# Decoder trunk on one core: dense tiles of 1408 and 1344 rows, B parts at other steps, half of a w_out product in three parts

## The reference

```
h = rmsnorm(x); z = h @ w_in            # 1024 -> 3 * 512
ya = S5 state-space mixer of z[:, :512] # B, C, recurrence, GELU, per-group GLU
yb = gated unit of z[:, 512:]
x = x + [rmsnorm(ya), rmsnorm(yb)] @ w_out
h = rmsnorm(x)
layer 1: x = x + (silu(h @ w_gate) * (h @ w_up)) @ w_down   # 2752 hidden
layer 2: x = x + top-2 of 8 experts, each a SwiGLU with 1376 hidden
```

## Time and profile before

| | us or share |
|---|---|
| median of the runs | 855.05 |
| the profiled execution, its own time | 856.37 |
| its span, from first to last instruction | 854.5 |
| TensorE (PE) busy | 812.2, 95% |
| VectorE (DVE) busy | 557.7, 65% |
| ScalarE (ACT) busy | 401.2, 47% |
| GpSimd (POOL) busy | 209.2, 24% |
| mean DMA rate | 235 GB/s |

### The profile page before, as it was taken

How to read it: one execution, slowest core, us unless ns; L and a number is a source line. 1 busy time by engine, 2 the same in 40 slices (tenths; PEclk the granted TensorE clock), 3 DMA queues, 4 the chain that set the end, 5 groups by cost and what they waited for, 6 DMA issues and landing times.

```text
span 854.5 us, 13785 instructions
## 1 busy us (share of the span) xinstructions
PE 812.2 (95%) x5080; PEld 631.7 (74%) x5080; DVE 557.7 (65%) x1006; ACT 401.2 (47%) x608; POOL 209.2 (24%) x182
## 2 busy tenths in 40 slices
PE   9999999999999969999999998998999998999994
PEld 7487779999999969848777887886876442865322
DVE  8999577566478871577952799799846131964115
ACT  7885455364332331377341587676734021750102
POOL 3801132223354111525112002414214000131002
PEclk9999999999999989999999899999999999999999
DMA  9603535554653431650410498987999999999993
GB/s 300 201 1 140 217 101 192 164 173 142 188 154 93 147 117 50 200 153 4 153 53 1 176 421 305 360 302 253 381 390 384 422 420 421 422 413 422 422 413 127
DMA packets 89474, 200.77 MB, mean 235 GB/s; under 512 B 26256, under 2 KB 48032, under 8 KB 89408
## 3 DMA queue, kind: packets, MB, share of 16 engines
q1 hardware_dynamic: 88480, 198.86, 63.5%
q10 hardware_dynamic: 576, 0.59, 0.2%
q0 software_dynamic: 352, 0.44, 0.2%
HBM read 198.25 MB, written 1.61 MB: 234 GB/s over the span
## 4 chain that ended last, share of the span: by engine, by line
PE 57%; DVE 20%; DMA 8%; issue 5%; SPq 5%; ACT 3%; POOL 1%; DVEq 0%; ACTq 0%; POOLq 0%
PE ps L1335 6%; PE ps L1336 6%; PE ps L1337 6%; PE ps L1539 5%; SPq L771 4%; PE ps L1345 4%; PE ps L1667 3%; PE ps L1651 3%; PE ps L1652 3%; PE ps L1654 3%; DVE D L1851 2%; DMA wraw_d<-in_moe_w_gate 2%; DMA wraw_g<-in_moe_w_down 2%; DMA wraw_g<-in_moe_w_gate 2%; PE ps L1429 2%
## 5 line engine op out<-in xcount | busy, mean ns | idle before, releaser
L1335 PE MATMUL ps<-Md,split_u 128*128 128x288 f32 (+2 forms) x304 | 89.7, 295 | 0.0
L1337 PE MATMUL ps<-Md,split_u 128*128 128x288 f32 (+2 forms) x304 | 89.1, 293 | 0.0
L1851 DVE TENSOR_TENSOR xb<-xb,ps 128x288 f32<-128x288 f32 x80 | 33.3, 450 | 70.8 <-PE ps L1539 26.6
L831 POOL TENSOR_TENSOR wrnd_g<-wraw_g,wrnd_g 128x1024 fp32r<-128x1024 f32 (+1 forms) x6 | 17.0, 2835 | 177.2 <-ACT wrnd_g L1012 177.2
L1851 DVE TENSOR_TENSOR wrnd_g<-wraw_g,wrnd_g 128x1376 fp32r<-128x1376 f32 (+2 forms) x31 | 48.9, 1597 | 13.8 <-ACT wrnd_g L1012 13.6
L1851 DVE TENSOR_TENSOR wrnd_u<-wraw_u,wrnd_u 128x1376 fp32r<-128x1376 f32 (+2 forms) x34 | 57.8, 1732 | 0.0
L1336 PE MATMUL ps<-hbr,split_u 128*128 128x288 f32 (+1 forms) x192 | 57.1, 297 | 0.0
L1337 PEld LDWEIGHTS ps<-Md,split_u 128*128 128x128 f32 (+2 forms) x304 | 56.9, 187 | 0.0
L1335 PEld LDWEIGHTS ps<-Md,split_u 128*128 128x128 f32 (+2 forms) x304 | 56.8, 187 | 0.1
L1851 DVE TENSOR_TENSOR wrnd_d<-wraw_d,wrnd_d 128x1376 fp32r<-128x1376 f32 (+2 forms) x20 | 31.8, 1620 | 34.1 <-ACT wrnd_d L1012 34.1
L1006 ACT ACTIVATE split_u<-raw 128x1024 fp32r<-128x1024 f32 (+2 forms) x38 | 39.5, 1047 | 30.0 <-PE ps L1337 30.0
(11 more groups left out here) (472 smaller groups left out, 2171.9 us busy)
## 6 DMA issues: line engine op xcount, KB each, us to landing
wraw_g<-in_moe_w_gate SPq DMA_DIRECT2D x31, 688.0 KB, 11.2
wraw_u<-in_moe_w_up SPq DMA_DIRECT2D x29, 688.0 KB, 17.0
wraw_d<-in_moe_w_gate SPq DMA_DIRECT2D x22, 688.0 KB, 9.1
wraw_g<-in_moe_w_down SPq DMA_DIRECT2D x28, 512.0 KB, 15.2
wraw_u<-in_moe_w_down SPq DMA_DIRECT2D x28, 512.0 KB, 13.7
raw<-in_ffn_w_gate SPq DMA_DIRECT2D x20, 512.0 KB, 4.6
raw<-in_ffn_w_up SPq DMA_DIRECT2D x20, 512.0 KB, 4.2
raw<-in_ffn_w_down SPq DMA_DIRECT2D x20, 512.0 KB, 3.8
```

The costliest lines, as they stand in the source:

```text
L1335: pe.matmul(out, w_hi, x_hi, start=start, stop=False)
L1337: return pe.matmul(out, w_lo, x_hi, start=False, stop=stop)
L1851: return dve.tensor_tensor(o, a, b, op)
```

## The change

- The first half of the hidden rows is 1408 (eleven full tiles), the second 1344 (ten and 64 rows). In the second half's last tile, gate and up weights stand side by side in one split slot (64 columns each) and go through one product of 128 output rows. VectorE takes the gate from partitions 0 to 63 and up from 64 to 127.
- In the last down chunk (64 rows) the high weights are copied a second time to partitions 64 to 127, and the low part of the hidden is put below its high part. One product then gives high x high and high x low, a second low x high.
- The B parts move from steps 41, 44, 45, 48, 49, 52, 53, 56 to 31, 33, 45, 66, 67, 68, 69, 70. Steps from 66 on have no chunk left to round.
- In layer 2, output tiles 4 to 7 of w_out are split products. ScalarE rounds that half of w_out (`out_high`, eight of 128x512) and the normalised y (`yn_high`), VectorE subtracts (`out_low`, `yn_low`), each at the places shown.

```diff
+LAST = 64
+HALF_AT = (0, FT * P)
-B_AT = (41, 44, 45, 48, 49, 52, 53, 56)
+B_AT = (31, 33, 45, 66, 67, 68, 69, 70)
+def rows(hf, kk):
+    return P if kk < FT - 1 else (P, LAST)[hf]
...
+        def dense_halves(n):
+            r, w = dense_chunk(n)[3:]
+            c = n - HALF_CHUNKS - 4 * MPAIRS
+            if c in (0, 1):
+                hi, lo = [a[:, 0:KT * P].rearrange("p (k f) -> p k f", f=P)[:, :, LAST * c:LAST * (c + 1)]
+                          for a in split_slot(n - c)]
+                return hi, lo, raw_slot(n)[:, 0:w].rearrange("p (k f) -> p k f", f=LAST)
...
 # ScalarE
             def high(n):
+                if n == DENSE - 1:
+                    act.activation(split_slot(n)[0][LAST:2 * LAST, 0:DM], src, ACT.Copy)
+                act.activation(hi, src, ACT.Copy).then_inc(hi_done, 1)
+            def out_high(k):
+                act.wait_ge(w_out_in[k // 2], 32)
+                act.activation(wo_h[:, k, :], w_out[:, k, MIX:DM], ACT.Copy).then_inc(hi_done, 1)
+            def yn_high(k):
+                act.wait_ge(h_ready, 24 + 8 + (k - MT if k >= MT else k + MT) + 1)
+                act.activation(yn_h[:, k, :], yn(k), ACT.Copy).then_inc(hh_ready, 1)
                 for q in range(MT):
                     if q == MT - 1:
                         squares(ub, h, MT, lambda k: act.wait_ge(yb_ready, 4 * l + k + 1))
+                        for k in range(2 if l else 0):
+                            out_high(k)
                     act.wait_ge(y_mm, 4 * l + q + 1)
                     act.activation(ua[:, q, :], bank((1, 2, 0, 1)[q]), ACT.Gelu_apprx_tanh).then_inc(y_ready, 1)
+                    if l and q == 1:
+                        for k in range(MT, KT):
+                            out_high(k)
                 root(4 * l + 1, 4, MIX, rs[:, T:2 * T])
                 for q in range(MT):
                     act.wait_ge(glu_mm, 4 * l + q + 1)
+                    if l and q == 2:
+                        for k in range(2, MT):
+                            out_high(k)
...
                 root(4 * l + 2, 3, MIX, rs[:, 0:T])
+                if l:
+                    for k in (*range(MT, KT), *range(MT)):
+                        yn_high(k)
 # TensorE, w_out
+                        if l and m >= 4:
+                            if m == 4 and k == 0:
+                                pe.wait_ge(lo_dve, lows_before(DENSE, False) + KT)
+                                pe.wait_ge(hl_ready, 2 * KT)
+                            f = slice((m - 4) * P, (m - 3) * P)
+                            mm = split_mm(bank(out_bank[m]), wo_h[:, k, f], wo_l[:, k, f], yn_h[:, k, :], yn_l[:, k, :],
+                                          k == 0, k == KT - 1)
 # TensorE, dense
+                            if hf and p == MPAIRS:
+                                wait_low(pe, n)
+                                wait_low(pe, n + 1)
...
+                                for k in range(KT):
+                                    mm = split_mm(bank(4 * (p % 2)), w_hi[:, k, :], w_lo[:, k, :],
+                                                  h_h[:, k, :], h_l[:, k, :], k == 0, k == KT - 1)
+                                mm.then_inc(chunk_used, 2)
...
+                                if r < P:
+                                    pe.matmul(bank(m), w_hi[:, f], hid_h[:, kk, :], start=False, stop=False)
+                                    mm = pe.matmul(bank(m), w_lo[0:r, f], hid_h[0:r, kk, :], start=False, stop=True)
 # VectorE
+                if n == 2 * MPAIRS + 1:
+                    link(tt(up, ps[r:2 * r, b0 - 2:b0 - 1, 0:T], r_ffn[r:2 * r, :].unsqueeze(1), ALU.mult))
...
+                if l:
+                    for n in range(MT):
+                        out_low(MT + n, n)
+                    for k in range(2):
+                        out_low(k, MT + k)
                 normalise(4 * l + 2, 1, [(yn(MT + k), ub[:, k, :], col(l, "out_norm_b", k)) for k in range(MT)])
...
+                for k in range(2, MT if l else 2):
+                    out_low(k, MT + k)
                 dve.wait_ge(ya_ready, 4 * (l + 1))
                 normalise(4 * l + 3, 0, [(yn(k), ua[:, k, :], col(l, "out_norm_a", k)) for k in range(MT)])
...
+                for n in range(MT if l else 0):
+                    yn_low(n)
...
+                        for n in range(2 * m + MT, 2 * m + MT + 2 if m < 2 else 0):
+                            yn_low(n)
```

## The result

The changed kernel takes 849.96 us, against 855.38 us for the kernel before in the same comparison: a ratio of 0.9928, with a 95% interval of 0.9909 to 0.9947. The forecast was 844.3, with a range from 841.0 to 848.5. The direction was right; of the 10.7 us expected about 6 came (5.4 in the medians, 6.2 by the ratio). The profiled execution took 849.6 us, its span 847.5.

A forecast was written before the change was run, and what follows sets the result against it. TensorE held 57% of the chain of waits, with a rigid, DMA-busy expert stage. Dense stage 10.5 us (4.2 + 9.8 - 3.5), plus 2.8, less 2.6, gave 10.7 us off 855.05: 844.3, range 841 to 848.5.

The forecast's parts named there:

- Fewer products: Dense stage, second half's narrower last tile: 32 fewer products at 0.1318 us, all on TensorE's path, 4.2 us won.
- packed products running at a pace of their own: Rival, dense stage: packed products do not run at the assumed pace; 4 us less gain, 848.3 us, chance 0.04.
- B parts, 9.8 us: Dense stage, second half: moving them removes two TensorE stops (0.91, 7.08), 0.32 of modelled idle and 1.4 of low clock.
- New stall: Second half's last tile: halved cover makes TensorE wait 2.3 us before the down products, then 1.15; 3.5 us lost.
- I take none: At the 2.3 us stop before the second half's down products: no clock fall was counted; 5 us stall if it falls.
- w_out, 2.8 us: Layer 2, output tiles 4 to 7: half of w_out as split products instead of full ones wins 2.8 us.
- Preparation, 2.6: Layer 2: ScalarE's copies and VectorE's differences for the split w_out products delay the chain by 2.6 us; bounds 0.6 and 5.
- (a): Before y's last GELU and first reciprocal: copies 0 and 1 await w_out's third piece, differences meet GpSimd's sums; 2.0 us lost.
- (b): On the way to the second reciprocal: two VectorE differences meet GpSimd's sums, one turn of 0.6 us lost.
- The expert stage as a rigid block: Second layer's experts, DMA busy 96%: the stage only shifts, so every microsecond won before it is won at the end.

The follow-up runs named there:

- full-row kernel: Changed kernel with the last down chunk's low product over all 128 rows, zeros below the 64 low weight rows: 845.59 us (0.9874), again 845.95 (0.9891).

## Why the prediction went wrong, by its own steps

- *Fewer products, 4.2 us.* This is the step that failed, in its last clause: "the down product takes 16 instead of 24", at 0.1318 us. It took 16 at 0.35 on average, 5.57 us instead of 2.11: 3.5 us, of which 3.0 are the alternation at full clock and 0.45 the lower clock at its end. The mechanism of the other 24 (gate and up in one product) was right. The 0.1318 us came from chunks without any change between 128 and 64 rows, and was put on products whose neighbours make that change each time. The Trainium skill has the rule (TensorEngine Tiling (Array Packing), Key Properties): changing the tiling mode, not just the tile, drains TensorE. The trace agrees for 64 and 128 rows, which behave as two such modes: 0.2 us more per change, in starts 0.33 us apart. Tiles of 96 rows next to full ones don't: in the kernel before, the first of them begins at 344.96, 0.13 us behind a full one. The rival of "packed products running at a pace of their own" came nearest, and looked at the wrong number: how many columns of output a product has, not how many rows it reads.
- *The clock,* a consequence that the sum did not have: 10.63 us for the first sixteen products of layer 2, against 8.61 in the full-row kernel, 2.0 us more (1.0 in the second profile of the changed kernel, whose chunk had lost more, 6.38 us). Together 5.4 us at the first means (351.79 against 346.37), 4.1 to 4.4 in the medians. That is nearly the whole distance between forecast and result (4.5 by the ratio, 5.3 by the medians): with full rows the ratio is 0.9874 and 0.9891, 9.3 to 10.8 us, against 10.7 predicted. That this range holds the 10.7 is in part luck: at the first filler the full-row kernel is 9.7 and 9.35 us ahead of the kernel before. The largest part that is missing there is the wait of layer 2 for h (next point); the whole times come up to 10.8 only with the scatter of the expert stage.
- *Hidden behind VectorE.* Even at full speed the eight products saved in the last chunk give little: the additions to x take 0.8 us per tile and start with the first tile's product, and layer 2 then waits for h. 0.85 of their 1.05 us is taken back (8.61 us to the first means instead of 7.76). The step that costed 32 products as all on TensorE's path should have stopped at 24.
- *B parts, 9.8 us:* 9.92 when alone. (The terms as given, 0.91, 7.08, 0.32 and 1.4, add up to 9.7.) Their new places cost nothing, as predicted: in the changed kernel five of them run from 320.17 to 331.4 and VectorE then idles 4.82 us before the first addition to x.
- *New stall, 3.5 us:* 3.6 (what its removal gave) to 3.9. It was 3.46 in the execution without a low clock behind it. "I take none" for the clock was wrong in seven profiles of nine, and cost 0.4 us where that bound had 1.5, since the slow products fill the second wait.
- *w_out, 2.8 us:* 2.55. *Preparation, 2.6:* 1.9, (a) about 1.4 of it and (b) about 0.5. Their mechanism was foreseen in part only. The last GELU ran 1.44 us after the end of its products (424.34 to 425.78) instead of 0.05: 1.4 late, not 1.8. The copies that waited for a load were 6 and 7, ahead of the GELU before (2.12 <-DMA, at 421.88), not 0 and 1; the squares of ub stand behind them. And hardly a turn was lost in (a): VectorE's differences ran from 422.55 to 423.84 and from 425.39 to 426.89, around GpSimd's two sums (424.08, 1.66 us, as before), and the reciprocal then waited for ScalarE. So (a) came out near its 2.0 by another path. In (b) the turns are there: two differences from 434.81 took 2.42 us beside GpSimd's sums from 434.69, where two alone take 1.29, and the sums took 1.99 instead of 1.67.
- *The expert stage as a rigid block:* right to within the scatter of single executions, some 3 us to either side.

The range ended at 848.5 because every doubtful cost had bounds except the one that was held for certain; the list of what the profile should show gave no number for the last chunk either.

What stays open: whether the clock falls because TensorE's load and product no longer overlap, or because of something else in the alternation. No kernel here lengthened the alternation or moved it elsewhere.

## What to carry to other kernels

A product's price belongs to its neighbours too: before a stationary tile of another height is put between full ones, look for a trace row in which the two kinds alternate, and if there is none, bound it by load plus pace instead of by the pace alone (here 0.18 + 0.13 us, and 0.33 was measured). Fill short tiles with zeros or group them by height; the zero rows cost nothing on TensorE (0.13 us per product with them). And when a step of an already long engine queue is merely moved, price it alone: here one line of placement brought 846.85 us, and the whole change with it 850.04.

## What the runs showed of the hardware

- Products of 288 columns over 64 rows run at 0.13 us among themselves, as over 128; each change between 64 and 128 rows costs 0.2 us (0.1 on leaving towards full products), and weights are no longer loaded one product ahead.
- Behind such an alternation the granted clock fell to its lower level, in three profiles of three, and without it in none of nine. Behind a stop of 2.3 us it fell in seven profiles of nine, and in one of the two of the changed kernel itself.
- Two VectorE differences of 128x512 take 1.29 us alone and 2.42 us beside two sums of GpSimd, which take 1.99 instead of 1.67.
